# Who issues the refills of the experts' down matrices: SyncE's list or ScalarE at each round's end

## The chip, the cores and the metric

One core of a Trainium2 chip runs the whole program. Its engines are TensorE (matrix multiplications, PE), VectorE (DVE), ScalarE (ACT), GpSimd (POOL) and SyncE (SP), which here only issues transfers. The time is device microseconds of one execution, lower is better. The kernel before took 1401.83 us (median of 3 runs, 1399.35 to 1402.54).

## The reference

Two layers. In each, a token mixer (causal pooling beside latent attention) and a mixture of experts, both with a residual and a layer norm. The expert part matters here: 256 tokens, width 1024, 64 routed experts of inner width 256, each token goes to 8 of them.

```python
def swiglu(x, w_gate, w_up, w_down):
    return (jax.nn.silu(x @ w_gate) * (x @ w_up)) @ w_down

for l in range(DEPTH):                       # 2 layers
    ...                                      # mixer, residual, layer norm
    idx, gates = route(ht, w_router, router_bias)      # top 8 of 64 experts
    ffn = swiglu(h, w_sh_gate[l], w_sh_up[l], w_sh_down[l]) \
        + sum over the chosen experts e of  gate_e * swiglu(h, w_gate[e], w_up[e], w_down[e])
    x = layer_norm(ALPHA * x + g2 * ffn, ...)
```

All is float32. One expert has a gate, an up and a down matrix of 1 MB each, so the 128 experts of the two layers are 384 MB of the 496 MB that are moved.

## The kernel before, in words

**Slots, pairs, rounds.** Six slots in SBUF hold one expert each. Two slots make a pair: pair 0 is slots 0 and 1, pair 1 is slots 2 and 3 (all four in the tensor `ring`), pair 2 is slots 4 (in `flex`) and 5 (in `w1`, printed as `w`). The experts are sorted by how many tokens they got, and worked through in 22 rounds a layer: two head rounds with a pair each, then 10 cycles of a quad round (four experts, pairs 2 and 0) and a pair round (two experts, pair 1). A round has as many blocks as its fullest expert needs, mostly one, in some two or three. A block gives each of the round's experts 32 token rows in a quad round and 64 in a pair round, so that all 128 rows of the array are in use.

**A block on TensorE.** The gate and up multiplications (L862, first half of the depth, then second half), the gather of the next block's tokens (L791), the turned middle (L871), the down multiplications (L878), the turning of the gathered tokens (L801) and the scatter into the accumulators (L899). The middle of the gate and up multiplications of a round's last matmuls is told by the semaphore `gu_half_done`, their end by `gu_done`, the end of the down multiplications by `down_done`. At a round's start TensorE waits for the first halves of gate and up of the round's pairs, in the middle for the second halves, and before the down multiplications for `down_landed`.

**ScalarE in a block** does silu (L1039), copies the gathered tokens out (L1019) and then the turned ones (L1025). At a round's start it reads from a table in SBUF (`btab`) where the round's blocks begin and end (two register loads, L364).

**The refills.** SyncE runs one list, in this order: for each pair that a round has finished, `refill` (from L509) reads the table and the two experts' numbers (three register loads), waits for `gu_half_done` and sends the first halves of gate and up (L424, four transfers of 512 KB), waits for `gu_done` and sends the second halves, waits for `down_done` and sends the two down matrices (L428, 1 MB each). In a cycle these are pair 2, pair 0 (both after the quad round) and pair 1 (after the pair round). Each transfer stands in SyncE's queue behind those issued before. The first experts of a layer are loaded by the same list before the rounds start.

Of the kernel before, what the change touches and what calls it, by code (L numbers as in the profile page):

```python
# [26 lines left out]
P = 128  # L27
# [28 lines left out]
HEAD = 2  # L56
CYCLES = 10
CYCLE = 6
NROUNDS = HEAD + 2 * CYCLES
# [79 lines left out]
def decoder_trunk(nc, x, c, positions, w_ada, b_ada, w_in, q_norm_g, kv_norm_g, w_uq, w_ukv, w_pool,  # L139
# [3 lines left out]
    ds = bass.ds  # L143

    with ExitStack() as ctx:
# [5 lines left out]
        def sem(name):  # L151
            return ctx.enter_context(nc.semaphore(name))
# [43 lines left out]
        def part_w(s, first, n):  # L196
            tensor, base = slot_at[s]
            return tensor[:, base + first:base + first + n]
# [7 lines left out]
        def down_w(s):  # L206
            return part_w(s, 2 * KT * F, KT * F).rearrange("p (k d) -> p k d", k=FT)
# [72 lines left out]
        def rt(i, n=NT * E):  # L280
            return temp[:, i:i + n]
# [21 lines left out]
        place = rt(1388, E)  # L303
# [47 lines left out]
        s = {n: sem(n) for n in names}  # L351
# [4 lines left out]
        down_landed = [sem(f"down_landed{i}") for i in range(SLOTS // 2)]  # L356

        def passed(eng):

            eng.sem_inc(s["waits_passed"], 1)  # L360

        def btab_value(eng, r):

            return eng.value_load(btab[0:1, ds(r, 1)], min_val=B0, max_val=MAXB)  # L364

        def blocks(eng, r):

            begin = btab_value(eng, r)
            return begin, btab_value(eng, r + 1)

        def placed(eng, place):

            return eng.value_load(otab[0:1, ds(place, 1)], min_val=0, max_val=E - 1)
# [14 lines left out]
        def _(sp):  # L388
# [29 lines left out]
            def load_gate_up(l, half, slots, experts):  # L418

                kts = slice(half * KT // 2, (half + 1) * KT // 2)  # L420
                for slot, e in zip(slots, experts):
                    for dst, w in ((gate_w, w_exp_gate), (up_w, w_exp_up)):
                        src = w[ds(l, 1), ds(e, 1)].rearrange("a b (p k) f -> p (a b k) f", k=KT)
                        sp.dma_start(dst(slot)[:, kts, :], src[:, kts, :]).then_inc(gu_landed[half][slot // 2], 16)  # L424

            def load_down(l, slots, experts):
                for slot, e in zip(slots, experts):
                    sp.dma_start(down_w(slot), w_exp_down[ds(l, 1), ds(e, 1)].rearrange("a b (k p) d -> p (a b k) d", p=P)).then_inc(down_landed[slot // 2], 16)  # L428
# [10 lines left out]
            for l in range(L):  # L439
# [3 lines left out]
                if l:  # L443
                    quads, used = btab_value(sp, NROUNDS - 1), btab_value(sp, NROUNDS)
# [66 lines left out]
                def refill(l, q, used_round, place):  # L511

                    used = btab_value(sp, used_round + 1)
                    experts = [placed(sp, place + g) for g in range(2)]
                    slots = (2 * q, 2 * q + 1)
                    sp.wait_ge(s["gu_half_done"], used)
                    passed(sp)
                    load_gate_up(l, 0, slots, experts)
                    sp.wait_ge(s["gu_done"], used)
                    passed(sp)  # L520
                    load_gate_up(l, 1, slots, experts)
                    sp.wait_ge(s["down_done"], used * 2)
                    passed(sp)
                    load_down(l, slots, experts)

                experts = [placed(sp, 2 * HEAD + g) for g in range(2)]
                for half in range(2):
                    load_gate_up(l, half, (4, 5), experts)
                load_down(l, (4, 5), experts)
                refill(l, 0, 0, 2 * HEAD + 2)  # L530
                refill(l, 1, 1, 2 * HEAD + 4)
                with sp.Fori(1, CYCLES) as i:
                    refill(l, 2, i * 2 + HEAD - 2, i * CYCLE + 2 * HEAD)
                    refill(l, 0, i * 2 + HEAD - 2, i * CYCLE + 2 * HEAD + 2)
                    refill(l, 1, i * 2 + HEAD - 1, i * CYCLE + 2 * HEAD + 4)
# [374 lines left out]
        def _(act):  # L910
# [16 lines left out]
            for l in range(L):  # L927
# [26 lines left out]
                for n in range(2, 12):  # L954
                    act.wait_ge(s["jobs_done"], l * 12 + n + 1)
                    b = ps[:, 2 + n % 6, :]
# [58 lines left out]
                def gathered(b, half):  # L1015

                    act.wait_ge(s["gath_done"], (b + l) * 2 + half + 1)
                    passed(act)
                    fn(G_sb[:, half * 512:(half + 1) * 512], ps[:, B_0 + half, :], ACT.Copy).then_inc(s["G_ready"], 1)  # L1019

                def gathered_T(b, half):

                    act.wait_ge(s["gT_done"], (b + l) * 2 + half + 1)
                    passed(act)
                    fn(hTb[:, 4 * half:4 * half + 4, :], ps[:, B_1 - half, :].rearrange("p (k n) -> p k n", k=4), ACT.Copy).then_inc(s["hT_ready"], 1)  # L1025
# [5 lines left out]
                    gathered_T(b0, half)  # L1031
                act.wait_ge(s["table_ready"], l + 2)
                passed(act)
                with act.Fori(0, NROUNDS) as r:
                    begin, end = blocks(act, r)
                    with act.Fori(begin, end) as b:
                        act.wait_ge(s["gu_done"], b + 1)
                        act.wait_ge(s["mid_ready"], b)
                        fn(sil, ps[:, B_F, 0:F], ACT.Silu).then_inc(s["sil_ready"], 1)  # L1039
                        for half in range(2):  # L1040
                            gathered(b + 1, half)
                        for half in range(2):
                            gathered_T(b + 1, half)
                total = btab_value(act, NROUNDS)
                for j in range(NT):
                    norm(1, j)
# [417 lines left out]
```

## Time and profile before

| | us |
|---|---|
| median of 3 runs | 1401.83 |
| the profiled execution | 1401.18 |
| its span | 1399.4 |
| TensorE busy | 1283.2 |
| VectorE busy | 466.2 |
| ScalarE busy | 247.6 |
| GpSimd busy | 158.6 |

496 MB are moved at a mean of 354 GB/s; all dynamic transfers are in one hardware queue (130496 packets, 495.17 MB). Most packets are of 4 KB. The experts of the first layer run from 197.96 to about 682 us, those of the second from 867.03 to about 1379 us. Times in the rows are us from the start of the span.

### The profile page before, as it was taken

What the parts mean: (1) busy time and instruction counts of PE and PEld (TensorE: products, weight loads), DVE (VectorE), ACT (ScalarE), POOL (GpSimd) and SP (SyncE); (2) the same over time, 40 slices, a digit from 0 to 9 for tenths busy, and PEclk for the clock granted to TensorE, in tenths of its full rate; (3) what the DMA queues carried; (4) which work ended last, traced back from release to release, by engine and by line L of the source; (5) the groups of instructions that cost most, each with busy time, mean ns of one, the idle gap of its engine ahead of it and who ended that gap; (6) DMA issues with size and microseconds to landing.
All of it is one profiled execution on the core that took longest, in us unless ns stands there. A gap on an engine that the chain in (4) does not pass through costs nothing.

```text
span 1399.4 us, 24090 instructions
## 1 busy us (share of the span) xinstructions
PE 1283.2 (92%) x7001; PEld 632.3 (45%) x7001; DVE 466.2 (33%) x1098; ACT 247.6 (18%) x511; POOL 158.6 (11%) x587
## 2 busy tenths in 40 slices
PE   3899999799799998999688999999999999989994
PEld 0465554344344443444246556444444444444441
DVE  1524543122222232233552354222332222323335
ACT  0133111011111111111112412111111111111111
POOL 0000022012011120121000002021111111201110
PEclk9999999999899999999889999999999999999997
DMA  9984959999999999999998395769989999999991
GB/s 348 381 346 159 368 185 410 409 409 409 409 409 409 409 409 409 375 367 410 397 384 315 129 356 189 306 241 405 409 331 410 409 409 409 409 409 388 376 410 59
DMA packets 130559, 496.08 MB, mean 354 GB/s; under 512 B 16168, under 2 KB 16176, under 8 KB 123840
## 3 DMA queue, kind: packets, MB, share of 16 engines
q1 hardware_dynamic: 130496, 495.17, 90.7%
q8 instruction: 48, 0.79, 0.2%
q14 instruction: 15, 0.12, 0.0%
HBM read 494.04 MB, written 1.08 MB: 354 GB/s over the span
## 4 chain that ended last, share of the span: by engine, by line
PE 81%; DVE 6%; DMA 5%; issue 3%; ACT 2%; SPq 2%; DVEq 0%; POOL 0%; ACTq 0%; POOLq 0%
PE ps L862 30%; PE ps L878 15%; PE ps L899 8%; PE ps L791 6%; DMA ring<-in_w_ada 5%; PE ps L801 4%; PE ps L724 4%; PE ps L595 2%; PE ps L871 2%; PE ps L747 2%; DVE w L1424 1%; DVE flex L1198 1%; PE ps L659 1%; PE ps L827 1%; ACT w L1039 1%
## 5 line engine op out<-in xcount | busy, mean ns | idle before, releaser
L862 PE MATMUL ps<-ring,w 128*64 128x512 f32 (+1 forms) x1888 | 424.5, 602 | 2.6 <-ACT w L1025 1.8
L878 PE MATMUL ps<-ring,w 128*64 128x512 f32 (+1 forms) x944 | 215.0, 597 | 0.0
L862 PEld LDWEIGHTS ps<-ring,w 128*64 128x64 f32 (+1 forms) x1888 | 131.7, 127 | 150.0 <-issue 150.0
L862 PE MATMUL ps<-flex,w 128*32 128x512 f32 x368 | 168.7, 612 | 29.0 <-issue 28.8
L1424 DVE SCALAR_TENSOR_TENSOR w<-ps,w 128x256 f32<-128x256 f32 x59 | 28.6, 484 | 422.8 <-ACT w L1039 422.8
L862 PE MATMUL ps<-w 128*32 128x512 f32 x368 | 169.2, 614 | 0.0
L791 PE MATMUL ps<-hx,scat 128*128 128x512 f32 x488 | 144.1, 417 | 0.9 <-issue 0.9
L1412 DVE CAST scat<-ps 128x512 fp32r<-128x512 f32 x118 | 81.6, 692 | 164.5 <-PE ps L878 164.5
L899 PE MATMUL ps<-scat 128*128 128x512 f32 x472 | 123.4, 403 | 0.0
L1039 ACT ACTIVATE w<-ps 128x256 f32<-128x256 f32 x59 | 22.8, 386 | 517.4 <-PE ps L862 517.4
L791 PEld LDWEIGHTS ps<-hx,scat 128*128 128x128 f32 x488 | 82.5, 188 | 60.7 <-issue 49.7
L1025 ACT ACTIVATE w<-ps 128x512 f32<-128x512 f32 x122 | 66.3, 596 | 237.3 <-PE ps L801 237.3
L1100 POOL CAST idg<-G 128x2 fp32r (+1 forms) x256 | 40.3, 189 | 559.8 <-PE ps L807 545.5
L862 PEld LDWEIGHTS ps<-flex,w 128*32 128x32 f32 x368 | 39.5, 113 | 133.0 <-issue 133.0
L1019 ACT ACTIVATE w<-ps 128x512 f32<-128x512 f32 x122 | 72.9, 598 | 109.8 <-PE ps L791 109.8
L899 PEld LDWEIGHTS ps<-scat 128*128 128x128 f32 x472 | 84.3, 189 | 15.5
L878 PEld LDWEIGHTS ps<-ring,w 128*64 128x64 f32 (+1 forms) x944 | 57.5, 126 | 64.4 <-issue 61.7
L878 PE MATMUL ps<-w 128*32 128x512 f32 x184 | 83.3, 595 | 0.0
L878 PE MATMUL ps<-flex,w 128*32 128x512 f32 x184 | 83.3, 595 | 0.0
L1414 DVE TENSOR_TENSOR scat<-ps,scat 128x512 fp32r<-128x512 f32 x118 | 81.6, 692 | 4.0
L801 PEld LDWEIGHTS ps<-const,w 128*128 128x128 f32 x488 | 52.4, 141 | 49.5 <-issue 49.5
L1404 DVE TENSOR_REDUCE w<-ps 32x1 f32<-32x4 f32 x244 | 38.5, 158 | 101.6 <-PE ps L899 96.9
(227 smaller groups left out, 1220.7 us busy)
## 6 DMA issues: line engine op xcount, KB each, us to landing
ring<-in_w_exp_gate SPq DMA_DIRECT2D x176, 512.0 KB, 13.8
ring<-in_w_exp_up SPq DMA_DIRECT2D x176, 512.0 KB, 14.5
ring<-in_w_exp_down SPq DMA_DIRECT2D x88, 1024.0 KB, 16.9
ring<-in_w_ada SPq DMA_DIRECT2D x48, 1024.0 KB, 10.1
flex<-in_w_exp_gate SPq DMA_DIRECT2D x40, 512.0 KB, 12.4
flex<-in_w_exp_up SPq DMA_DIRECT2D x40, 512.0 KB, 13.1
w<-in_w_exp_gate SPq DMA_DIRECT2D x40, 512.0 KB, 13.5
w<-in_w_exp_up SPq DMA_DIRECT2D x40, 512.0 KB, 15.2
```

What stands on the lines that cost most here:

```text
L724: last = mm(acc3[:, j, half, :], xT3[:, kt, j * P:(j + 1) * P], wout3[:, kt, half * 512:(half + 1) * 512], start=kt == 0, stop=kt == KT - 1)
L791: last = mm(ps[:, B_0 + half, :], S[:, j, :], part[:, j, q], start=j == 0 and part is hx_hi, stop=j == NT - 1 and part is hx_lo)
L801: last = tr(ps[:, B_1 - half, k * P:(k + 1) * P], G_sb[:, c * P:(c + 1) * P], ident)
L862: last = mm(ps[unit * g:unit * g + unit, B_F, :].rearrange("p (q f) -> p q f", q=2), hTb[:, kt, unit * g:unit * g + unit], gate_up(k)[:, : ...
L878: last = mm(ps[unit * g:unit * g + unit, bank, :], midT[:, f, unit * g:unit * g + unit], down_w(k)[:, f, half * 512:(half + 1) * 512], sta ...
L899: last = mm(acc3[:, j, half, :], ST[:, j * P:(j + 1) * P], part[:, half * 512:(half + 1) * 512], start=False, stop=True, skip_group_check= ...
L1019: fn(G_sb[:, half * 512:(half + 1) * 512], ps[:, B_0 + half, :], ACT.Copy).then_inc(s["G_ready"], 1)
L1025: fn(hTb[:, 4 * half:4 * half + 4, :], ps[:, B_1 - half, :].rearrange("p (k n) -> p k n", k=4), ACT.Copy).then_inc(s["hT_ready"], 1)
L1100: eng.tensor_copy(slot_gates[j][:, :, cols], G2[:, :, j, ds(e, 1)].to_broadcast([P, 2, width]))
L1412: v.tensor_copy(hi, ps[:, bank, :]).then_inc(s["hi_ready"], 1)
L1414: return v.tensor_tensor(lo, ps[:, bank, :], hi.bitcast(F32), ALU.subtract)
L1424: v.scalar_tensor_tensor(mid, ps[:, B_F, F:2 * F], gslot, sil, ALU.mult, ALU.mult).then_inc(s["mid_ready"], 1)
```

## The change

The wait for `down_done` and the down transfers leave SyncE's list. ScalarE's loop over the rounds is written out as `one_round`, and after each round that frees a pair ScalarE runs `refill_down`: three register loads, the wait for `down_done`, and the two down transfers, from ScalarE's own queue. After a quad round it does so for pair 2 and then for pair 0. The first down matrices of a layer are still loaded by SyncE.

```diff
@@ SyncE, refill()
                     sp.wait_ge(s["gu_done"], used)
                     passed(sp)
                     load_gate_up(l, 1, slots, experts)
-                    sp.wait_ge(s["down_done"], used * 2)
-                    passed(sp)
-                    load_down(l, slots, experts)
@@ ScalarE
-                with act.Fori(0, NROUNDS) as r:
+                def one_round(r):
+
                     begin, end = blocks(act, r)
...
+                def refill_down(q, used_round, place):
+
+                    used = btab_value(act, used_round + 1)
+                    experts = [placed(act, place + g) for g in range(2)]
+                    act.wait_ge(s["down_done"], used * 2)
+                    passed(act)
+                    for slot, e in zip((2 * q, 2 * q + 1), experts):
+                        act.dma_start(down_w(slot), w_exp_down[ds(l, 1), ds(e, 1)].rearrange("a b (k p) d -> p (a b k) d", p=P)).then_inc(down_landed[slot // 2], 16)
+
+                one_round(0)
+                refill_down(0, 0, 2 * HEAD + 2)
+                one_round(1)
+                refill_down(1, 1, 2 * HEAD + 4)
+                with act.Fori(1, CYCLES) as i:
+                    one_round(i * 2 + HEAD - 2)
+                    refill_down(2, i * 2 + HEAD - 2, i * CYCLE + 2 * HEAD)
+                    refill_down(0, i * 2 + HEAD - 2, i * CYCLE + 2 * HEAD + 2)
+                    one_round(i * 2 + HEAD - 1)
+                    refill_down(1, i * 2 + HEAD - 1, i * CYCLE + 2 * HEAD + 4)
+                one_round(NROUNDS - 2)
+                one_round(NROUNDS - 1)
```

SyncE's list in the loop over the cycles, before: from the second half of gate and up of pair 2 to the first transfers of pair 0.

```order
L424 ISA [waits gu_done]
L424 DMA flex<-in_w_exp_gate 128x1024
L424 DMA flex<-in_w_exp_up 128x1024
L424 ISA
L424 DMA w<-in_w_exp_gate 128x1024
L424 DMA w<-in_w_exp_up 128x1024
L522 REGISTER_ALU
L428 DMA flex<-in_w_exp_down 128x2x1024 [waits down_done]
L428 DMA w<-in_w_exp_down 128x2x1024
L364 TENSOR_LOAD btab
```

The same place now:

```order
L424 ISA [waits gu_done]
L424 DMA flex<-in_w_exp_gate 128x1024
L424 DMA flex<-in_w_exp_up 128x1024
L424 ISA
L424 DMA w<-in_w_exp_gate 128x1024
L424 DMA w<-in_w_exp_up 128x1024
L364 TENSOR_LOAD btab
```

The two down matrices and their wait are gone, so the list goes on to pair 0 at once.

ScalarE at the end of a quad round in the loop, now, from the last copy of the block to the next round's first register load (before, only the two rows of the branch stood between them; the numbers of the lines are those of the changed kernel):

```order
L1022 ACTIVATE w<-ps 128x512 [waits gT_done] x2
L1034 REGISTER_ALU
L1034 COMPARE_AND_BRANCH
L364 TENSOR_LOAD btab
L364 ISA x2
L373 ISA
L373 TENSOR_LOAD otab
L373 ISA x3
L373 TENSOR_LOAD otab
L373 ISA x2
L1047 REGISTER_ALU
L1050 ISA [waits down_done]
```

```order
L1050 DMA flex<-in_w_exp_down 128x2x1024
L1050 ISA
L1050 DMA w<-in_w_exp_down 128x2x1024
L364 TENSOR_LOAD btab
L364 ISA x2
L373 ISA
L373 TENSOR_LOAD otab
L373 ISA x3
L373 TENSOR_LOAD otab
L373 ISA x2
L1047 REGISTER_ALU
L1050 ISA [waits down_done]
```

The second piece follows the first without a gap, and two more DMA rows, into `ring`, follow it. So six register loads, two waits and four transfers stand before the next round's two loads and its silu.

## Rows read from the trace of the kernel before

**Rows 1.** The page's slices, 40 of 35 us: clock, transfer share, rate.

```profile
PEclk9999999999899999999889999999999999999997
DMA  9984959999999999999998395769989999999991
GB/s 348 381 346 159 368 185 410 409 409 409 409 409 409 409 409 409 375 367 410 397 384 315 129 356 189 306 241 405 409 331 410 409 409 409 409 409 388 376 410 59
```

**Rows 2.** Busy time by stretch, granted clock, transfer share and rate.

```profile
core 0: us, PE busy (x) PEld busy (x) DVE busy (x) ACT busy (x) POOL busy (x), PEclk, DMA share, GB/s
230.53:271.89 41.36, 32.45 (x201) 15.16 (x201) 10.51 (x27) 5.33 (x10) 5.78 (x24) 0.95 1.03 409
...
1210.58:1246.80 36.22, 32.43 (x202) 15.17 (x201) 10.52 (x27) 5.34 (x10) 4.96 (x18) 1.00 1.03 409
```

**Rows 3.** Chain of waits, whole span: start, us, what; quads after two-block cycles.

```profile
263.12 8.78 issue
271.89 8.42 PE ps L862 x64
...
354.38 9.61 issue
...
543.82 5.91 issue
549.74 9.44 PE ps L862 x64
...
1063.73 7.08 PE ps L862 x64
...
1243.19 3.61 issue
1246.80 8.80 PE ps L862 x64
```

**Rows 4.** Chain of waits, 925 to 975: one two-block cycle and the next quad.

```profile
932.15 7.11 PE ps L862 x64
...
941.81 0.20 PE ps L807 x2
...
948.46 7.10 PE ps L862 x32
...
964.76 3.61 PE ps L862 x32
968.37 0.91 issue
```

**Rows 5.** SyncE's issues in that cycle: start, us, what.

```profile
929.42 0.91 SPq L428 DMA_DIRECT2D ring<-in_w_exp_down  x2
...
936.05 0.34 SPq L424 DMA_DIRECT2D flex<-in_w_exp_gate  x1
...
945.76 0.38 SPq L428 DMA_DIRECT2D flex<-in_w_exp_down  x1
946.23 0.42 SPq L428 DMA_DIRECT2D w<-in_w_exp_down  x1
948.78 0.35 SPq L424 DMA_DIRECT2D ring<-in_w_exp_gate  x1
...
955.50 3.11 SPq L428 DMA_DIRECT2D ring<-in_w_exp_down  x2
```

**Rows 6.** Line 424, 946 to 956: issue to landing of pair 0's eight transfers.

```profile
DMA to landing us min/median/max: 8.4/12.0/15.1
```

**Rows 7.** ScalarE's timeline at the end of that quad round.

```profile
946.29 1.09 ACT L1025 ACTIVATE w<-ps 128x512 f32<-128x512 f32 x2 [3.76 <-PE ps L801]
955.58 0.39 ACT L1039 ACTIVATE w<-ps 128x256 f32<-128x256 f32 x1 [8.21 <-PE ps L862]
```

**Rows 8.** Line 364 on ScalarE, 245.5 to 248: one round's two loads.

```profile
L364 ACTq TENSOR_LOAD <-btab x2: 280/280/281, 245.5 to 246.1; - x2
```

**Rows 9.** Line 428 on SyncE, whole span: ns min/median/max of an issue.

```profile
L428 SPq DMA_DIRECT2D ring<-in_w_exp_down x88: 378/1509/2801, 139.4 to 1351.8; - x88
```

## The prediction, made before the changed kernel had run

> **What bounds the kernel now.** I read the page's slices first, then the chain of waits, then the stretches where that chain has idle pieces, and last SyncE's list of transfers beside them. In the slices [rows 1] the two expert stages (slices 6 to 19 and 27 to 38, counted from 0) show a transfer share of 9 tenths nearly throughout, 409 GB/s in most, and, in the page's line for it, a TensorE at 9 tenths as well: the two run at almost the same pace. A quad round followed by a pair round refills six experts of 3 MB each (3.15 million bytes), 18.9 MB, which at 0.409 MB per us is 46.1 us. A block takes 16.3 us on TensorE (932.15 to 948.46 to 964.76, [rows 4]). So a cycle of three blocks (48.9 us) leaves transfers a little time and a cycle of two blocks (32.6 us) falls short by 13.5 us. In the chain of waits [rows 3] TensorE stands still only at the quad round that follows a two-block cycle: 8.78 us before 271.89, 9.61 us before 364.00, 5.91 us before 549.74, 3.61 us before 1246.80, and 0.91 us in the middle of the quad at 964.76 [rows 4]. Two more quads follow a two-block cycle without a wait, the one at 1063.73 [rows 3] and its like in the first layer. The stretches [rows 2] show what these waits are: over 230.53 to 271.89 and over 1210.58 to 1246.80 the engines of the DMA moved 409 GB/s without a gap. So the bound is the order and the start of transfers against these seven deadlines, and every late byte there is paid in full.
>
> Each long wait also costs clock: in the stretch of 230.53 to 271.89 the granted clock is 0.95 of full [rows 2], and the gate and up multiplications behind the wait took 8.42 us instead of 7.08 [rows 3], 1.3 us more.
>
> **What one deadline looks like before.** Take the cycle at 932.15 [rows 4, 5]. Two halves of 2.1 MB of gate and up for pair 2 start at 936.05, its down matrices (2.1 MB) at 945.76, the halves for pair 0 at 948.78, its downs at 955.50. Up to pair 0's second half that is 10.5 MB; at 0.409 it has passed at 936.05 + 25.7 = 961.7. It is needed at 968.37 and was there at 969.28 (the last of it, issued at 954.1, took 15.1 us [rows 6]). So the last parts of a transfer trail the sum of bytes by 7.6 us; I carry that lag over.
>
> **What changes, part by part.** Removed from SyncE per refill: one wait for down_done and two issues of about 0.4 us each (946.23, [rows 5]). The wait goes: SyncE can send pair 0's first half about 2.1 us of register loads (946.65 to 948.78) after pair 2's second half, near 943.5 instead of 948.78. That by itself moves no more bytes, since in the first expert cycles the transfers had no gap, and in this one 4.2 MB of gate and up (10.3 us from 936.05, so to 946.3) cover the wait that ended at 945.76. I put it at 0. What is late next is the transfers' rate.
>
> Added on ScalarE: after the last activation of a round, three register loads and two issues per pair, two pairs after a quad round. ScalarE's last activation in the quad's block starts at 946.29 and lasts 1.09 [rows 7]; with SyncE's 2.1 us for the loads, plus the start, the downs of pair 2 leave near 949.5 instead of 945.76, those of pair 0 near 952.7 instead of 955.50, and those of pair 1, after a pair round, near 932.9 instead of 929.42. Behind them on ScalarE stands the next block's silu, for which VectorE and then TensorE wait. Its room is the idle time of 8.21 us before 955.58 [rows 7]; the work is 2 x (2.1 + 0.9) + 1.2 for the two table loads of the next round, 0.6 us apart [rows 8], so 7.2 us. It fits with 1 us to spare, cost 0; if an issue lasts as long as SyncE's median of 1.51 us for such a matrix [rows 9], four issues add 4.4 us and each quad round's end is 3.4 us late.
>
> The term that counts is the order. There are now two queues. No row shows two at once, so I bound it from both sides. The same cycle again: pair 1's downs start at 932.9 and by 936.05 have moved 1.3 of 2.1 MB, 0.8 are left. From there to 949.5, 13.45 us move 5.5 MB: those 0.8 and 4.7 MB of gate and up. 3.7 MB of gate and up remain when 4.2 MB of downs arrive on the other queue. If both advance equally, gate and up end at 949.5 + 3.7 / 0.2045 = 967.6, with the lag 975.2, against a need of 968.37: 6.8 us late where 0.91 was. If everything is served in order of issue, gate and up are in time, but all the bytes have passed at 949.5 + 7.9 / 0.409 = 968.8, the downs are there at 976.4, and the first down multiplications want them 9.7 us after the block's start (941.81 - 932.15), at 974.4: 2.0 us late, and 5.1 us more if pair 1's first half (2.1 MB, released in the pair's block near 952) slips ahead of pair 0's downs. If the downs' queue gets more than half, pair 1's next downs also pass ahead, 5.1 us on top of 6.8. The three outcomes are all on the late side, because the sum of bytes is unchanged and the downs of pairs 1 and 2 start 3.5 to 3.7 us later. I take equal advance, the middle one.
>
> The Trainium skill, "DMA: Bandwidth & Descriptors", section "Queues, rings and completion order", says that each DMA engine takes turns between the queues with work, packet by packet; by it the equal split holds and the sum is the one below, while in order of issue it would be near 1420. No row of this one-queue trace shows it.
>
> **The sum.** Seven deadlines:
> - 271.89 and 364.00: transfers never pause from the start of the stage, so only the shift of order counts once: 2.1 MB more ahead of the last gate and up half, 5.1 us.
> - 549.74: before it 5.91 + (9.44 - 7.08) = 8.3 us [rows 3]; after it 6.8 + 1.3 of clock = 8.1, and with what the shift leaves I take +1.
> - The like of 1063.73 in the first layer: 0 before, 8.1 after.
> - 964.76: 0.9 before, 8.1 after, +7.2.
> - 1063.73: 8.1.
> - 1246.80: 3.61 + (8.80 - 7.08) = 5.3 before, 8.1 after, +2.8.
> - The two last quads of the second layer come one pair block after a quad round of two blocks. There pair 1's downs are long through: 2.9 MB remain at the split, 14.2 us, ending at 31.6 after the quad's start, 39.2 with the lag, needed at 36.2: 3.0 each, 6.0.
> Together 38 us. The profiled execution took 1401.2 (span 1399.4), the median of the runs is 1401.8, so both give about 1439.
>
> **The rivals.**
> 1. In order of issue: at three deadlines without a wait before, 2.0 to 7.1 us, small amounts at the others, about +18: 1420. For it: the descriptors of a deep SyncE list might be fetched first. Against it: they lie in different queues.
> 2. Faster, because gate and up pass the downs. The place is the quad at 1246.80. Before, a quad can start when 10.5 MB are there less 3.6 us; after, when 12.6 MB are there less 9.7 us, which is 5.1 later less 6.1, so 1.0 us earlier. At the four long waits and the short one this gives back 5 us: 1396. It decides itself at the downs' issue: as soon as they start over 1.0 us later than before, the gain is gone, and they start 3.7 later; it needs the lag of 7.6 us to shrink as well.
> 3. ScalarE is late: its issues last 1.5 us, 3.4 us at each of 18 quad ends with refills, 61 us, of which a third falls into waits for data: 1439 + 41 = 1480. Against it: its queue would hold at most 6.3 MB in 48 us and is never as deep as SyncE's.
> 4. The downs' queue gets two thirds: 7 x 5.1 = 36 more, 1475.
> 5. Nothing changes, if both effects cancel or the lag hides in the slack: 1401.
>
> The same page's section "Issuing engines are not separate DMA queues" says that a second issuing engine saves only the time of issuing. Here SyncE's issuing is on no part of the chain, which by that rule leaves no gain: it lowers rival 2.
>
> **How the numbers follow.** Forecast 0.50, in order of issue 0.25, faster 0.07, ScalarE late 0.08, two thirds 0.06, nothing 0.04. What a measurement here can tell from no change is about 0.2%, 3 us. Of rival 1's quarter 0.04 lies within that or below (0.03 and 0.01). So faster 0.08, same 0.07, slower 0.85. The range from 1406 to 1468 leaves out faster, same and a little below, and rivals 3 and 4 above; it holds 6.8 us at each deadline being as little as 2.0 or as much as 11.
>
> **What would show it.** Right: two transfer queues in the profile, the second with 122 MB (29 refills of two matrices in each of two layers, 1.05 MB each); idle pieces of 5 to 8 us in or before the quads after two-block cycles, also in the two places that had none; waits in the middle of the gate and up multiplications rather than before them; 9 tenths of transfers as before. ScalarE's idle before the silu shrinks to about 1 us after a quad round, and the silu is not late. Wrong: gate and up in time at those quads (rival 2), TensorE waiting at the down multiplications (rival 1), or a silu after its gu_done by more than 0.5 us at many round ends (rival 3).

## The result, and the profile after

The changed kernel takes 1428.47 us (median of 4 runs, 1424.66 to 1430.51) against 1400.59 (median of 4, 1398.73 to 1402.54): 1.020 times the time before, 95% interval 1.0183 to 1.0218, so 28 us slower. The forecast was 1439 with a range of 1406 to 1468. The profiled execution took 1430.51 us, its span is 1428.7.

The page after, with the slices that answer to [rows 1] and the queues:

```profile
PEclk9999999799999999999899999999999999999997
DMA  9975869999999999899898577499799999998990
GB/s 354 387 316 175 338 234 409 409 409 409 409 409 410 408 391 410 327 355 401 350 363 341 177 285 286 178 371 409 295 372 409 409 409 409 386 390 321 352 386 30
...
q1 hardware_dynamic: 98944, 373.53, 67.4%
q10 hardware_dynamic: 31552, 121.64, 21.5%
```

ScalarE's queue q10 carries the 122 MB of down matrices. The rate in the full slices is the same 409 GB/s, and VectorE's and ScalarE's busy times are as before; TensorE is busy for 1295.6 us instead of 1283.2, at a mean granted clock of 0.962 instead of 0.970. A few slices of the expert stages that held 409 before are lower now (391 in slice 14, 386 and 390 in slices 34 and 35, counted from 0).

The chain of waits, whole span, the idle pieces and what follows them, against [rows 3, 4]. L859 is the gate and up line of the changed kernel ("issue" marks idle time for which the profile shows no releaser; these pieces stand where the program waits for its matrices):

```profile
279.54 5.20 PE ps L859 x32
...
364.16 3.64 PE ps L859 x32
367.80 6.57 issue
374.36 5.61 PE ps L859 x32
...
551.35 3.61 PE ps L859 x32
554.96 4.60 issue
559.56 5.13 PE ps L859 x32
...
654.94 3.62 PE ps L859 x32
658.56 4.42 issue
662.98 6.32 PE ps L859 x32
...
969.86 3.62 PE ps L859 x32
973.47 5.77 issue
979.25 5.25 PE ps L859 x32
...
1078.86 5.82 issue
...
1265.89 5.55 issue
...
1322.87 2.04 issue
...
1373.93 3.40 issue
```

The waits stand at the quads that the prediction named, the two without a wait before among them (654.94 and 1078.86), and, from the second on, no longer ahead of the block but in its middle: 3.6 us after its start, where the second halves of gate and up are needed. The last two are the quads one pair block behind a quad round of two blocks. Only the first, at 279.54, still begins late (32.1 us after the pair before it, of which a block takes 16.2). Its row in TensorE's timeline gives the wait, 15.85 us where it was 8.78:

```profile
279.54 1.03 PE L859 MATMUL ps<-flex,w 128*32 128x512 f32 x1 [15.85 <-DMA ring<-in_w_exp_up]
```

What happened to the transfers shows in SyncE's issues after the quad at 937.26, with ScalarE's issues of the down matrices ("the downs") beside them (start, us, what). The first two rows are the last of pair 0's second halves, the others are pair 1's gate and up:

```profile
952.92 0.64 SPq L424 DMA_DIRECT2D ring<-in_w_exp_gate  x1
953.65 0.99 SPq L424 DMA_DIRECT2D ring<-in_w_exp_up  x1
...
958.89 2.05 SPq L424 DMA_DIRECT2D ring<-in_w_exp_gate  x1
961.04 2.31 SPq L424 DMA_DIRECT2D ring<-in_w_exp_up  x1
963.60 1.98 SPq L424 DMA_DIRECT2D ring<-in_w_exp_gate  x1
...
966.75 5.98 SPq L424 DMA_DIRECT2D ring<-in_w_exp_gate  x1
```

```profile
954.03 0.39 ACTq L1050 DMA_DIRECT2D flex<-in_w_exp_down  x1
954.58 0.38 ACTq L1050 DMA_DIRECT2D w<-in_w_exp_down  x1
957.06 0.93 ACTq L1050 DMA_DIRECT2D ring<-in_w_exp_down  x2
960.68 0.39 ACT L1037 ACTIVATE w<-ps 128x256 f32<-128x256 f32 x1 [8.21 <-PE ps L859]
...
970.33 0.93 ACTq L1050 DMA_DIRECT2D ring<-in_w_exp_down  x2
```

With room in the queue an issue takes 0.33 to 0.38 us; the longer ones are taken here as waiting until the queue has drained far enough. Before, in the same cycle, such an issue was

```profile
954.09 1.18 SPq L424 DMA_DIRECT2D ring<-in_w_exp_up  x1
```

for 512 KB, close to the 1.28 us that 0.52 MB take at 409 GB/s. While ScalarE's four matrices are under way three in a row last 2.0 to 2.3 us (others there 0.9 and 6.0). The queues themselves show it directly. From the start of the quad to the end of its wait, 969.83 to 979.25, ScalarE's q10 and SyncE's q1 carried (packets, MB, share)

```profile
q10 hardware_dynamic: 515, 1.98, 52.4%
q1 hardware_dynamic: 517, 1.87, 50.1%
```

so SyncE's queue has half of the rate. The core as a whole is not slower: in the stretch of the quad that waited (us, busy times, clock, transfer share, GB/s) it moves 410 GB/s,

```profile
969.83:993.84 24.01, 17.98 (x126) 7.47 (x125) 4.73 (x11) 2.67 (x5) 1.66 (x3) 0.86 1.03 410
```

so the other half goes to the down matrices, which are needed only at the down multiplications, at 987.25. The second halves of pair 0, issued before ScalarE's first down matrix, were therefore awaited until 979.25, 9.4 us after the quad's start, against 4.5 before (969.28 less 964.76, [rows 4]).

### The profile page after: what moved, and what is told of

The parts are those of the page before. It is cut to its first block, busy times and chain, and to the rows that moved or that the text cites. A ratio compares the mean times of both kernels' runs of the same rounds, so it can differ in the third digit from the quotient of the medians.

```text
span 1428.7 us, 24752 instructions
## 1 busy us (share of the span) xinstructions
PE 1295.6 (91%) x7001; PEld 632.8 (44%) x7001; DVE 466.2 (33%) x1098; ACT 247.7 (17%) x511; POOL 158.6 (11%) x587
## 4 chain that ended last, share of the span: by engine, by line
PE 77%; DVE 9%; issue 5%; DMA 4%; SPq 3%; ACT 2%; DVEq 0%; POOL 0%; ACTq 0%; POOLq 0%
PE ps L859 30%; PE ps L875 14%; PE ps L896 7%; PE ps L788 5%; PE ps L798 4%; PE ps L721 4%; DMA ring<-in_w_ada 2%; DVE flex L1218 2%; DMA ring<-in_w_exp_up 2%; PE ps L868 2%; PE ps L744 2%; DVE w L1444 1%; PE ps L656 1%; SPq L424 1%; PE ps L824 1%
## 5 line engine op out<-in xcount | busy, mean ns | idle before, releaser
L859 PE MATMUL ps<-ring,w 128*64 128x512 f32 (+1 forms) x1888 | 434.4, 612 | 2.1 <-ACT w L1022 1.8
L859 PE MATMUL ps<-flex,w 128*32 128x512 f32 x368 | 178.4, 637 | 56.6 <-issue 40.4
L875 PE MATMUL ps<-ring,w 128*64 128x512 f32 (+1 forms) x944 | 215.0, 597 | 0.0
L859 PEld LDWEIGHTS ps<-ring,w 128*64 128x64 f32 (+1 forms) x1888 | 132.3, 129 | 149.6 <-issue 149.6
L859 PE MATMUL ps<-w 128*32 128x512 f32 x368 | 179.1, 639 | 0.0
L859 PEld LDWEIGHTS ps<-flex,w 128*32 128x32 f32 x368 | 40.1, 116 | 169.7 <-issue 169.7
L875 PE MATMUL ps<-flex,w 128*32 128x512 f32 x184 | 83.3, 595 | 0.0
L875 PE MATMUL ps<-w 128*32 128x512 f32 x184 | 83.3, 595 | 0.0
```

The costliest lines, as they stand in the source:

```text
L859: last = mm(ps[unit * g:unit * g + unit, B_F, :].rearrange("p (q f) -> p q f", q=2), hTb[:, kt, unit * g:unit * g + unit], gate_up(k)[:, : ...
L875: last = mm(ps[unit * g:unit * g + unit, bank, :], midT[:, f, unit * g:unit * g + unit], down_w(k)[:, f, half * 512:(half + 1) * 512], sta ...
```

## The experiments

Three theories of where the 28 us come from. Theory A: the second queue takes half the rate, so down matrices pass gate and up that stood ahead of them. Theory B: the gate and up that SyncE now sends early do harm, or (B2) the downs start too late. Theory C: ScalarE's added work delays its silu.

### One queue, the changed kernel's order

```diff
-                    sp.wait_ge(s["down_done"], used * 2)
-                    passed(sp)
-                    load_down(l, slots, experts)
+                    held.append((slots, experts))
+                    if downs:                       # False for pair 2
+                        sp.wait_ge(s["down_done"], used * 2)
+                        passed(sp)
+                        for sl, ex in held:
+                            load_down(l, sl, ex)
+                        held.clear()
```

> SyncE issues everything, in one queue, but in the changed kernel's order of bytes: after a quad round gate and up of pair 2, gate and up of pair 0, and then the four down matrices at down_done. Theory A (the second queue takes half the rate while gate and up are still on the way): no loss, since nothing passes the gate and up halves: a quad after a two-block cycle then needs 12.6 MB by the down multiplications (9.7 us in) instead of 10.5 MB by the middle of gate and up (3.6 us in), 1.0 us earlier per deadline that waits, so 1 to 5 us faster than before: 1397 to 1400. Theory B (the early gate and up transfers, sent before the downs, are what hurts): as slow as the changed kernel, near 1428. Theory C (ScalarE's added work): equal to before, 1400.6.

Measured: 1403.32 us, ratio 1.0011 (0.9997 to 1.0026). No loss clear of noise, but no gain either, so above the 1397 to 1400 of theory A. The chain of waits tells why, in its first cycle:

```profile
263.93 2.86 issue
266.79 10.03 PE ps L868 x64
...
280.08 2.40 issue
282.92 5.27 PE ps L884 x32
```

The quad starts at 266.79, 5.1 us earlier than the 271.89 before, as 2.1 MB less stand ahead of it; then it waits before the down multiplications (L884) for the last down matrix. The deadline moved, and the sum of bytes met it at the same time: the down multiplications start at 282.92, where before they started at 283.05. After the second wait they also take 5.27 us instead of 3.57.

### The same, with the down matrices as late as ScalarE sends them

```diff
-                        sp.wait_ge(s["down_done"], used * 2)
+                        sp.wait_ge(s["scat_done"], used)
```

> As one_list, but the down matrices wait for scat_done, the end of the block, 2.8 us after down_done and within 1 us of when ScalarE issues its first down matrix in the changed kernel. The bytes and their times are those of the changed kernel, the second queue is not there. Theory A: near before, 1399 to 1404. Theory B2 (the downs simply start too late, in whatever queue): most of the 28 us, 1415 to 1428, with waits at the down multiplications (L878) of quads after two-block cycles.

Measured: 1405.26, ratio 1.0023 (1.0011 to 1.0035), 3 us, 1 us above theory A's range. B2 falls for the most part: the later start is worth about 3 of the 28 us. It is not quite the changed kernel's: there pair 0's downs leave 3.0 us after pair 2's (957.06 after 954.03), here all four are issued one behind the other.

### ScalarE's work without its transfers

The changed kernel with SyncE's three lines put back and this left out:

```diff
-                    for slot, e in zip((2 * q, 2 * q + 1), experts):
-                        act.dma_start(down_w(slot), w_exp_down[...]...).then_inc(down_landed[slot // 2], 16)
```

> ScalarE does all that the changed kernel gives it (three register loads and the wait for down_done per pair, the unrolled rounds) except the transfers; SyncE issues the down matrices as before. Theory A: ScalarE's added work costs nothing, equal to before, 1401 to 1404. Theory C (ScalarE's work at a round's end delays the silu): a visible part of the 28 us, 5 or more.

Measured: 1400.48, ratio 0.9993 (0.9983 to 1.0003). The loads and the wait cost nothing.

### Twice as many issues on ScalarE

```diff
-                        act.dma_start(down_w(slot), ...).then_inc(down_landed[slot // 2], 16)
+                        for f in range(FT):
+                            act.dma_start(down_w(slot)[:, f:f + 1, :], src[:, f:f + 1, :]).then_inc(down_landed[slot // 2], 16)
```

(SyncE's first ones likewise, and TensorE waits for 64 instead of 32.)

> The changed kernel with each down matrix in two transfers of 512 KB, so that ScalarE issues eight after a quad round instead of four. Bytes, times and queues are the same. In the changed kernel the last of four issues ends about 958.0, the next round's loads 1.3 us later, and the silu begins at 960.68: 1.4 us of room; four more issues of 0.5 us use 2.0, so the silu is late by 0.6 us at 18 quad ends, up to 10 us. Theory A: +0 to +10 over the changed kernel (1428 to 1438). If ScalarE's issues had no room already in the changed kernel (theory C), each added issue counts in full at all quad ends: +36 (1464).

Measured: 1428.67, ratio 1.0202 (1.0181 to 1.0224), the changed kernel's time. ScalarE's timeline at a quad round's end:

```profile
951.32 0.85 ACTq L1054 DMA_DIRECT2D flex<-in_w_exp_down  x2
952.34 0.84 ACTq L1054 DMA_DIRECT2D w<-in_w_exp_down  x2
955.26 1.90 ACTq L1054 DMA_DIRECT2D ring<-in_w_exp_down  x4
958.56 0.38 ACT L1039 ACTIVATE w<-ps 128x256 f32<-128x256 f32 x1 [8.79 <-PE ps L861]
```

The silu is late by 0.6 us (8.79 idle instead of 8.21), as worked out, so the room of the four issues was real and is used up by eight. In the total it does not show; that a TensorE held up by 0.6 us waits that much less for its data afterwards would explain it, and was not shown. Theory C falls.

### SyncE keeps its wait

```diff
                     load_gate_up(l, 1, slots, experts)
+                    sp.wait_ge(s["down_done"], used * 2)
+                    passed(sp)
```

> The changed kernel with SyncE still waiting for down_done after each pair's gate and up, as before, though it issues no down matrices: so gate and up of the next pair start when they did before. Theory A: the loss stays or grows a little, +25 to +38 (1427 to 1440), since the early gate and up were never the cause and a later start leaves more of pair 0's bytes to share the rate with the downs. Theory B (early gate and up hurt): back near 1402.

Measured: 1432.07, ratio 1.0224 (1.0196 to 1.0252). Gate and up sent as late as before, and 31 us lost instead of 28: theory B falls. The early issue helps by 3 to 4 us, which is within what the two intervals leave open.

### One part alone

The changed kernel with SyncE's three lines kept for all pairs but those named, and `refill_down` returning at once for the others:

```diff
+                    if q not in (1,):          # or (2, 0), (2,), (0,)
+                        sp.wait_ge(s["down_done"], used * 2)
+                        passed(sp)
+                        load_down(l, slots, experts)
...
                 def refill_down(q, used_round, place):
+                    if q not in (1,):
+                        return
```

Pair 1:

> Only pair 1's down matrices, after pair rounds, are issued by ScalarE; those of pairs 2 and 0 stay in SyncE's list. Theory A: pair 1's next downs start at the quad's first matmuls and meet the following gate and up; before a quad after a two-block cycle they have 3 us or so alone, then take half the rate for some 2 us; SyncE's list also holds pair 2's downs ahead of pair 0's gate and up as before. I expect about half to three quarters of the loss, +14 to +24 (1415 to 1425), since 2.1 MB pass gate and up that need not. Theory C (ScalarE's loads and issues): one third of the loss, +9, as it has one third of the issues.

Pairs 2 and 0:

> The other part alone: ScalarE issues the downs of pairs 2 and 0 after a quad round, SyncE those of pair 1. Theory A: 4.2 MB at half rate beside the rest of pair 0's gate and up, but the residue of pair 1's downs is gone: +10 to +18 (1411 to 1419). Theory C: two thirds of the loss, +19, and all of it at quad rounds' ends, with a silu that starts late.

Measured: pair 1 alone 1417.03, ratio 1.0119 (1.0097 to 1.0141); pairs 2 and 0 alone 1422.25, ratio 1.0158 (1.0137 to 1.0178). The first, 15 to 17 us, is in its range and above theory C's 9; the second, 20 to 22 us, is above mine and at theory C's number. Together they do not settle it, and by their ratios they add up to 39 (by the medians 35.5), more than the 28 of both. The two losses overlap; a likely reason is that a late deadline delays the releases behind it, and with them the next transfers, but no run separates that. So I took pairs 2 and 0 apart.

> ScalarE issues pair 2's down matrices alone, two after each quad round; SyncE the others. They start 3.6 us later than before and in a second queue. Theory A (what counts is the bytes that pass gate and up which were ahead of them before): before, pair 2's downs already stood ahead of pair 0's gate and up in SyncE's list, so nothing new passes; between -2 and +4 (1399 to 1405). Any theory by which a second queue as such, the later issue, or ScalarE's share of the work costs time gives about what the other pairs cost, +10 to +20.

> The mirror image: pair 0's down matrices alone on ScalarE, the same number of transfers by the same engine at the same round ends. Before they stood behind pair 0's gate and up; now 2.1 MB of them take half the rate while those are under way: up to 5.1 us later at each of the seven deadlines, and pair 1's gate and up, not held behind them any more, take their part. Theory A: +12 to +24 (1413 to 1425), at least three times pair2_act's loss. Theory C: the same as pair2_act.

Measured: pair 2 alone 1401.81, ratio 1.0007 (0.9997 to 1.0016); pair 0 alone 1421.99, ratio 1.0140 (1.0116 to 1.0165). The same number of transfers, from the same engine at the same places, after the same rounds: nothing for the one and 21 us for the other. The quad that follows the two-block cycle, in the chain of waits, with pair 2's downs on ScalarE:

```profile
966.84 3.64 PE ps L863 x32
970.48 1.12 issue
971.60 3.68 PE ps L863 x32
```

and with pair 0's:

```profile
969.70 3.95 issue
973.65 9.76 PE ps L863 x64
```

The first is the wait of before (0.91, [rows 4]). In the second the quad waits 3.95 us ahead of gate and up, and its multiplications take 9.76 us instead of 7.09. That is clock, not a second wait: they follow each other without a gap, at a granted clock of 0.72. The chain of waits of that kernel has such a wait, 2.8 to 12.2 us, at every one of the seven quads that the prediction named; with pair 2's downs on ScalarE the quad at 1067.07, the place of 1063.73 before, still has none. Pair 2's downs always stood ahead of pair 0's gate and up in the list, so on a queue of their own they pass nothing; pair 0's stood behind them and now pass. A second queue, a later start and ScalarE's hands are the same in both, so none of them alone is the cause. One thing does differ: with pair 2's downs gone from the list, SyncE sends pair 0's gate and up 11.3 us after the quad's start instead of 16.6. By the run that kept SyncE's wait this is worth 3 to 4 us, not 20.

### An attempt at a faster one

```diff
+                for half in range(2):
+                    q = slice(half * 512, (half + 1) * 512)
                     for slot, e in zip(slots, experts):
-                        sp.dma_start(down_w(slot), src).then_inc(down_landed[slot // 2], 16)
+                        sp.dma_start(down_w(slot)[:, :, q], src[:, :, q]).then_inc(down_landed[half][slot // 2], 16)
...
                         down(0, B_0)
+                        for q in pairs:
+                            pe.wait_ge(down_landed[1][q], loads[q] * 32)
                         down(1, B_F)
```

> An attempt at a faster one: one_list with the down matrices sent by column halves, the first halves of all four experts before the second ones, and TensorE waiting for the second halves only between the two down multiplications, 1.8 us later. In one_list a quad after a two-block cycle ends up waiting for its last down matrix. With this the last 2.1 MB are needed 1.8 us later: up to 1.8 us less at each of four waiting quads, 1395 to 1400. Against it: rows of 2 KB instead of 4 KB may lower the rate below 409 GB/s, and then it is slower than one_list.

Measured: 1407.62, ratio 1.0047 (1.0032 to 1.0062), slower than before. Over 260 to 360 us, the first row is of the one-queue kernel in the changed kernel's order, the second of this one:

```profile
DMA packets 11019, 40.87 MB, mean 409 GB/s; under 512 B 1053, under 2 KB 1053, under 8 KB 11015
```

```profile
DMA packets 14088, 40.17 MB, mean 402 GB/s; under 512 B 1223, under 2 KB 1223, under 8 KB 14083
```

The rate is 7 GB/s lower, with the DMA engines busy throughout. It goes with the rows of 2 KB and not with the number of transfers: the kernel with twice as many issues on ScalarE, whose down matrices are also sent in 512 KB but in rows of 4 KB and from two queues, holds 409 GB/s over the same stretch. Over a stage of about 200 MB at full rate the 7 GB/s would be an estimated 8 us, more than the 1.8 us per deadline could return. There is a second candidate that no run separates from it. SyncE's issues of 512 KB in rows of 2 KB last 1.8 us in the median, with many at 2.15, against the 1.18 of the row at 954.09 for 512 KB in rows of 4 KB. SyncE's issues make up 27% of this kernel's chain of waits and 2% of that of the one-queue kernel, so they may hold up gate and up by themselves. No version here beats the kernel before.

## Why the prediction was right, and by how much it was off

**The bound and the places** were right: transfers against the deadlines of quads after two-block cycles, and each named place shows its wait.

**The terms**, from the block starts in the two chains of waits, compared from one block after a deadline to one block after the next, in us:

| deadline (before) | predicted | measured |
|---|---|---|
| 271.89 and 364.00 | +5.1 | +7.5 |
| 549.74 | +1 | -2.0 |
| its like at 649.43 in the first layer | +8.1 | +7.3 |
| between the layers | 0 | -7.7 |
| 964.76 | +7.2 | +6.4 |
| 1063.73 | +8.1 | +7.8 |
| 1246.80 | +2.8 | +2.5 |
| the two last quads, 1297 and 1346 | +6.0 | +7.6 |
| sum | +38 | +29.4 |

(The spans differ by 29.3.) The mechanism's own terms sum to 38.3 predicted and 37.1 measured. That this sum is off by only 1.2 us is in part luck: single terms are off by up to 3.0, in both directions. The first deadline alone cost 9.2 us and the second gave 1.7 back, where one shift of 5.1 was said; the one at 549.74 gave 2.0 back instead of costing 1. Of the idle pieces, said to be 5 to 8 us, the first is 15.85 and two are 4.4 and 4.6.

At the deadline of 964.76 the size can be followed. Waits of 5.8 us in the middle and 1.6 us more for the second half's multiplications (5.25 instead of 3.67) make 7.4 at 973.47, where 8.1 was said, less the 0.9 of before. The clock term of 1.3 came out as 1.6, at a granted clock of 0.86.

**The term that was missing** is the one between the layers. The prediction's sum counted nothing outside the expert stages. There the next layer's first modulation matrices (`w_ada`) stand in SyncE's list behind the last refills. Before, TensorE was done with the last scatter at 681.9 and waited 11.07 us for them; after, it is done at 694.7, the transfers have come forward in the meantime, and it waits 6.23. TensorE's timeline, before and then after:

```profile
696.94 1.94 PE L566 MATMUL ps<-ring,c 128*32 128x512 f32 x8 [11.07 <-DMA ring<-in_w_ada]
```

```profile
704.52 1.94 PE L563 MATMUL ps<-ring,c 128*32 128x512 f32 x8 [6.23 <-DMA ring<-in_w_ada]
```

With the shorter waits behind these, TensorE stands 15.4 us before and 7.8 after at this line, 7.5 less, which is the term of -7.7 in the table. A wait for data in front of a stage that itself waits for data was partly paid back here. No run tested this by itself. This term is nearly the whole distance between the forecast and the result.

**The lag of 7.6 us** was carried over as if the last parts of a transfer always trailed by it. The trace before does not bear this out. Between 936.05 and 945.76 the transfers did not run at 409 GB/s but at 326, as SyncE's list stood at its wait for `down_done` (columns as in [rows 2]):

```profile
936.05:945.76 9.71, 9.62 (x78) 3.91 (x71) 2.41 (x5) 1.58 (x3) 3.01 (x14) 1.00 0.94 326
```

That is 2.0 of the 7.6 us. From then to the landing at 969.28 the rate was 408, so 12.8 MB moved in all, 2.3 MB (5.5 us) more than the 10.5 counted. Part of these were older: pair 1's two down matrices, issued from 929.42, landed 7.5 and 9.5 us after their issue, so behind 936.05. How much is left for a true trailing is open. After the change the list no longer stands at that wait, so the 2.0 us should be gone there; that the whole 7.6 served well all the same is in part luck.

**Equal advance** of the two queues, taken as the middle of three, was right: 517 packets of one and 515 of the other in the 9.4 us from the quad's start to the end of its wait, and SyncE's issues of 512 KB lasted 2.0 to 2.3 us instead of 1.18. The Trainium skill's rule ("DMA: Bandwidth & Descriptors", "Queues, rings and completion order": each DMA engine takes turns between queues) agrees with these numbers.

**The room on ScalarE** was right: predicted 1 us to spare, measured from 957.99 (the last issue's end) to 960.68, less 1.2 for two loads, 1.5 us. Its issues last 0.38 to 0.5 us each although SyncE's queue is full, so the fear of 1.5 us was unfounded. At 970.33 ScalarE issued two matrices in 0.93 us while SyncE stood in a single issue from 966.75 to 972.73: the backlog of the one queue did not hold the other's issues. The silu is not late (8.21 idle in [rows 7] and now). The prediction's sign for it, an idle time that shrinks to about 1 us, was badly put: register loads and issues do not count as busy, so the row cannot show it.

**The removed wait at 0** was about right. The prediction's reason was not: it had 4.2 MB of gate and up cover the old wait, but the rate was 326 GB/s there, and with the early issue it is 396 (941.15 to 949.30). The kernel in which SyncE keeps its wait, against the changed kernel (1432.07 to 1428.47), puts the early issue at 3.6 us in its favour, and the two intervals overlap, so that nothing at all is not excluded.

**Rival 2** (a gain of 1.0 us per deadline from order alone) could be tried in the one-queue kernel, where nothing speaks against it, and gave none (1403.32 against 1401.90 before). In the changed kernel it was buried anyway.

## What to carry to other kernels

When transfers are the bound, a list in the order of need was worth more here than early issue: moving some of them to a second queue gave these half the rate at once, at the cost of whatever was ahead of them. Ask of every transfer that changes queue what it will now pass; if it passes nothing (pair 2 here) the move is free, and if it passes something with an earlier deadline the price at each tight deadline is at most its bytes over the rate (for pair 0 that is 5.1 us at seven deadlines, 36 us, of which 21 were paid). And follow a delay to the next stage: some of it may come back there.

## What the runs showed of the hardware

- Two full hardware queues shared the core's transfer rate about equally (517 and 515 packets, 1.87 and 1.98 MB in 9.42 us), and their sum stayed at 409 to 410 GB/s.
- An issue on the emptier queue took about 0.5 us (two in 0.93) while one on the full queue lasted 5.98.
- With rows of 2 KB instead of 4 KB in a third of the bytes the rate was 402 instead of 409 GB/s; transfers of the same 512 KB in rows of 4 KB kept 409.
- Matrix multiplications behind a wait ran at a lower granted clock: 0.72 over the gate and up multiplications of 9.76 us that follow 3.95 us of idle time, which take 7.1 us at 1.00.
- A landing is not told by the sum of the bytes issued since some moment: pair 0's second halves were there at 969.28, 7.6 us after the 961.7 of that sum, with a rate of 326 instead of 409 GB/s in its first 9.7 us and older transfers still under way at its start.
